# A fused encoder layer on one core: the order of the first transposes, of the first projection halves and of the parameter loads

## What is computed

```python
u = x @ w_in[l]                      # (1024 x 1024) @ (1024 x 7688)
ua, ub, uc, ug = _split(u, GROUP_COLS)
oa = _gdn_branch(ua, ...)            # gated delta rule, chunks of 64
ob, v_first = _rwkv7_branch(ub, ...) # RWKV-7 time mixing
oc = _swa_branch(uc, ...)            # sliding-window attention
merged = gates * (oa @ w_branch_a, ob @ w_branch_b, oc @ w_branch_c), summed
x = _layer_norm(ALPHA * x + merged @ w_out[l], ln1_w[l], ln1_b[l])
x = _layer_norm(ALPHA * x + (silu(x @ ffn_gate) * (x @ ffn_up)) @ ffn_down, ln2_w[l], ln2_b[l])
```

## Time and profile before

| | us |
|---|---|
| median of 3 runs | 2105.22 (2103.75 to 2105.71) |
| profiled execution, its time | 2102.6 |
| its span, first to last instruction | 2100.8 |
| TensorE busy | 1967.7 (94%) |
| VectorE busy | 1078.3 (51%) |
| ScalarE busy | 567.8 (27%) |
| GpSimd busy | 558.6 (27%) |
| mean granted TensorE clock | 0.974 of full speed |

### The profile page before, as it was taken

One profiled execution on the slowest core, in us unless ns is written; L12 is line 12 of the kernel. 1 busy time (PEld: TensorE's weight loads), 2 busy tenths in 40 slices (PEclk: granted clock), 3 DMA queues, 4 the chain that ended last, 5 costly groups with the idle time before them and its releaser, 6 DMA issues. The chain is left out here.

```text
span 2100.8 us, 29168 instructions
## 1 busy us (share of the span) xinstructions
PE 1967.7 (94%) x11664; PEld 1575.3 (75%) x11664; DVE 1078.3 (51%) x1354; ACT 567.8 (27%) x884; POOL 558.6 (27%) x353
## 2 busy tenths in 40 slices
PE   5998979999999999899888999999999999999994
PEld 4876758767788887777767777888888888888883
DVE  3665764468429900566657644724334243443437
ACT  2443332334421121333331121321121211212112
POOL 3111112121122322433314473422121221212113
PEclk9999989999999999899999999999999999999997
DMA  5243566135563393566464461211121211211002
GB/s 144 53 70 89 130 151 164 51 76 140 148 173 100 97 218 107 147 189 197 119 215 131 134 207 51 61 61 50 41 60 30 60 32 58 60 30 60 30 20 80
DMA packets 328054, 211.84 MB, mean 101 GB/s; under 512 B 154349, under 2 KB 298349, under 8 KB 325905
## 3 DMA queue, kind: packets, MB, share of 16 engines
q1 hardware_dynamic: 251760, 156.33, 27.3%
q10 hardware_dynamic: 75568, 54.04, 9.0%
q0 software_dynamic: 624, 0.05, 0.2%
HBM read 151.27 MB, written 59.06 MB: 100 GB/s over the span
## 5 line engine op out<-in xcount | busy, mean ns | idle before, releaser
L154 PE MATMUL bank<-xhi,w_hi 128*128 128x512 f32 x976 | 396.3, 406 | 2.9 <-DVE xlo L920 2.9
L155 PE MATMUL bank<-xlo,w_hi 128*128 128x512 f32 x976 | 387.6, 397 | 0.0
L156 PE MATMUL bank<-xhi,w_lo 128*128 128x512 f32 x976 | 387.0, 397 | 0.0
L432 POOL TENSOR_TENSOR w_lo<-w_raw,w_hi 128x1024 fp32r<-128x1024 f32 x61 | 163.3, 2678 | 640.5 <-ACT w_hi L783 640.5
L2212 DVE TENSOR_TENSOR bw_raw<-bw_raw,b_ps 128x512 f32<-128x512 f32 x42 | 28.9, 688 | 388.3 <-PE b_ps L156 380.0
L154 PEld LDWEIGHTS bank<-xhi,w_hi 128*128 128x128 f32 x976 | 184.9, 189 | 49.0 <-issue 3.5
L155 PEld LDWEIGHTS bank<-xlo,w_hi 128*128 128x128 f32 x976 | 185.0, 190 | 44.7 <-issue 2.4
L156 PEld LDWEIGHTS bank<-xhi,w_lo 128*128 128x128 f32 x976 | 184.6, 189 | 45.0
L2220 DVE TENSOR_TENSOR y<-y,f_ps 128x512 f32<-128x512 f32 x320 | 201.0, 681 | 0.7
L1755 POOL TENSOR_TENSOR bw_split<-ff_raw_down,ff_hi_down 128x1024 fp32r<-128x1024 f32 x22 | 53.4, 2426 | 527.3 <-ACT ff_hi_down L2013 527.3
L154 PE MATMUL f_ps<-ff_hi_down,ff_hhi 128*128 128x512 f32 x352 | 142.7, 405 | 3.6 <-DVE ff_hlo L2231 3.6
(11 more groups left out here) (324 smaller groups left out, 3462.6 us busy)
## 6 DMA issues: line engine op xcount, KB each, us to landing
w_raw<-in_w_in ACTq DMA_DIRECT2D x61, 512.0 KB, 4.2
op<-opnd SPq DMA_DIRECT2D x16, 1152.0 KB, 5.5
u<-work ACTq DMA_DIRECT2D x68, 256.0 KB, 4.1
b_gate<-u SPq DMA_DIRECT2D x24, 512.0 KB, 3.6
ff_raw_gate<-in_ffn_gate SPq DMA_DIRECT2D x22, 512.0 KB, 4.0
ff_raw_up<-in_ffn_up SPq DMA_DIRECT2D x22, 512.0 KB, 5.3
ff_raw_down<-in_ffn_down SPq DMA_DIRECT2D x22, 512.0 KB, 5.9
opnd<-work SPq DMA_DIRECT2D x20, 512.0 KB, 6.2
```

Source lines behind the costliest of these rows:

```text
L154: pe.matmul(out, w_hi, x_hi, start=first, stop=False)
L155: pe.matmul(out, w_hi, x_lo, start=False, stop=False)
L156: return pe.matmul(out, w_lo, x_hi, start=False, stop=last)
L432: pool.tensor_tensor(w_lo[b][:, :, :], w_raw[b][:, :, :], as_f32(w_hi[b][:, :, :]), ALU.subtract).then_inc(w_lo_done, 1)
```

## The change

On TensorE the first token half is transposed per token tile, each when it has landed, and only the last tile counts `turned`. `dense(0)` follows at once and waits for `xlo` block by block. The second half is transposed between `dense(0)` and `dense(1)`, in banks 3 to 7 only (`second_bank`), as banks 0 to 2 belong to the halves. On ScalarE `split(0)` moves ahead of all copies, and the second w tile's load behind `split(0)`. The 17 parameter loads move from GpSimd's queue to SP's, between x and the tables, and the tables get a semaphore of their own.

```diff
+        second_bank = lambda k: turn_bank[3 + k % 5]
...
-        rows_landed = sem("rows_landed")
+        rows_landed, tables_landed = sem("rows_landed"), sem("tables_landed")
...
         @block.gpsimd
         def _(pool):
-            nonlocal par_loads
-            par_loads = load_params(nc, pool, par, A, par_landed)
             for m in range(NT_IN):
...
-            pool.wait_ge(par_landed, par_loads)
             local.sweep(pool)
...
             for i in range(4, 8):
                 load_x(i)
-            sp.dma_start(tab.tile[:, P:], const_dram[:, P:N_TABLES]).then_inc(const_landed, 16)
+            par_loads = load_params(nc, sp, par, A, par_landed)
+            sp.dma_start(tab.tile[:, P:], const_dram[:, P:N_TABLES]).then_inc(tables_landed, 16)
             prep()
+            sp.wait_ge(par_landed, par_loads)
...
                 for k in range(KT):
+                    if q < 2:
+                        pe.wait_ge(x_lo_done, 8 * q + k + 1)
                     last = split_dot(pe, bank[to % 3][:, :], w_hi[b][:, k, :], w_lo[b][:, k, :],
...
             pe.wait_ge(const_landed, 16)
-            for n in range(16):
-                half, k = n // 8, n % 8
-                if k == 0:
+            for i in range(4):
+                pe.wait_ge(x_landed[i], 16)
+                for k in range(KT):
+                    last = pe.transpose(turn_bank[k][:, i * P:(i + 1) * P], work[:, i, k * P:(k + 1) * P], tab("ident"))
+                    if i == 3:
+                        last.then_inc(turned, 1)
+
+            def turn_second_half():
+                for i in range(4, 8):
+                    pe.wait_ge(x_landed[i], 16)
+                for k in range(KT):
+                    pe.wait_ge(x_lo_done, k + 4)
                     for i in range(4):
-                        pe.wait_ge(x_landed[4 * half + i], 16)
-                if n >= 8:
-                    pe.wait_ge(x_lo_done, n - 7)
-                for i in range(4):
-                    last = pe.transpose(turn_bank[n % 8][:, i * P:(i + 1) * P], work[:, 4 * half + i, k * P:(k + 1) * P], tab("ident"))
-                last.then_inc(turned, 1)
-            pe.wait_ge(x_lo_done, 16)
+                        last = pe.transpose(second_bank(k)[:, i * P:(i + 1) * P], work[:, 4 + i, k * P:(k + 1) * P], tab("ident"))
+                    last.then_inc(turned, 1)
...
                     dense(item)
+                    if item == 0:
+                        turn_second_half()
...
             load_w(0)
+            split(0)
             load_w(1)
             for n in range(16):
                 half, k = n // 8, n % 8
                 act.wait_ge(turned, n + 1)
-                act.activation(xhi[:, k, half * HALF:(half + 1) * HALF], turn_bank[n % 8], ACT.Copy).then_inc(x_hi_done, 1)
-                if n == 11:
-                    split(0)
+                act.activation(xhi[:, k, half * HALF:(half + 1) * HALF], second_bank(k) if half else turn_bank[k], ACT.Copy).then_inc(x_hi_done, 1)
             split(1)
...
-            dve.wait_ge(const_landed, 32)
+            dve.wait_ge(const_landed, 16)
+            dve.wait_ge(tables_landed, 16)
```

More of the change, by code:

```diff
@@ L571, in prep @@
                             sp.dma_start(out[:, :, which, 2 * r + pp, :], tile[64 * pp:64 * pp + 64, r, :, :]).then_inc(inv_stored, 16)
+            nonlocal par_loads
             load_x(0)
@@ L919, in _ @@
                 dve.wait_ge(x_hi_done, n + 1)
-                dve.tensor_tensor(xlo[:, k, cols_], turn_bank[n % 8], as_f32(xhi[:, k, cols_]), ALU.subtract).then_inc(x_lo_done, 1)
+                dve.tensor_tensor(xlo[:, k, cols_], second_bank(k) if half else turn_bank[k], as_f32(xhi[:, k, cols_]), ALU.subtract).then_inc(x_lo_done, 1)
             step(dve.memset(raws[:, :, 0:3], 0.0))
```

## The result

The changed kernel's median is 2083.56 us (2082.00 to 2084.76, four runs); the kernel before stood at 2104.49 beside it. The ratio is 0.9907 (95% interval 0.9895 to 0.9918): 0.93%, which is 19.6 us of 2104.49. (The two medians differ by 20.9 us, which the interval holds too.) The forecast was 2087.7 in a range from 2084 to 2097. The direction and the mechanism held and the gain was larger than forecast: the median of 2083.56 lies 0.4 us under the lower edge of the range, while the same ratio on the forecast's own base, 0.9907 x 2105.22 = 2085.6, lies inside it. The profiled execution's span went from 2100.8 to 2082.2.

The account below looks back on a forecast made before the run. TensorE, busy 94% of the span, was taken as the bound, its start waiting for x; q0 at 12.8 plus 5.6, 1.2 cold and 9.6 put q2 at 29.2 for 46.66, saving 17.5 us: 2087.7, range 2084 to 2097.

Parts of the forecast that it names:

- Arrival of x: Start of the kernel: with parameters behind x, tile 3 lands at 10.3 us and tile 7 at 16.7.
- own time only: Rival on x's landing: parameters cost x only their own 3.2 us; gain 13.1 us, 2092.1; chance 0.16.
- arrival unchanged: Rival on x's landing: x lands as before; gain 8.3 to 9.8 us, about 2096; chance 0.10.
- q0's start: First projection half on TensorE: starts at 12.8 us for 35.36, chosen between first x_lo (12.2) and w_lo (13.3).
- The term ahead of it: Transposes after x tile 3: ScalarE's first copy needs one transpose, not four; 0.5 us for 1.12.
- The clock: First projection half on TensorE: 1.2 us added for a part at 1.2 GHz, between nothing and 2.2.
- The second half's turn: Second token half's transposes, between the first two projection halves: q1 starts 4.0 us after q0 ends.
- The second w split: ScalarE and GpSimd ahead of q2: second w_lo is ready with 0.7 us to spare.
- Parameters late: Parameter loads on SP's queue behind x tile 7: landed at 28 us, ScalarE waits 2 us, no cost.
- a sign that it is wrong: Parameters on ScalarE: the forecast is wrong if ScalarE waits beyond 30 us for them.
- T + 9.7: ScalarE's next evacuation, by which it must be free of the parameter wait; T is q0's end, 19.6 us.
- 43: Rival on late parameters: landing between 43 and 53 us eats the gain to nothing; chance within 0.2%: 0.05.

Follow-up runs that it names:

- GpSimd experiment: Kernel before, with GpSimd waiting for all eight x tiles before it issues the parameter loads through its own queue; ratio 0.9999 (0.9989 to 1.0008).
- new order alone: Changed kernel with its parameter loads back on GpSimd's queue at the start; ratio to the kernel before 0.9949 (0.9935 to 0.9962), 10.7 us faster.
- tables experiment: Changed kernel with the tables ahead of the parameters on SP's queue; ratio to the kernel before 0.9908 (0.9893 to 0.9923).
- doubled loads: Changed kernel with every parameter load done twice on SP's queue; ratio to the kernel before 0.9982 (0.9973 to 0.9991), 3.8 us faster.
- first experiment: Kernel before with only the parameter loads moved to SP's queue behind x; ratio 0.9945 (0.9931 to 0.9958), 11.6 us faster.

## Why the prediction was right, point by point

- **Arrival of x.** 10.3 and 16.7 were forecast, 10.2 and 15.8 came. The reading of the earlier trace rows, that the parameters make x's rows dear, is shown by the GpSimd experiment, where they alone were moved in time. The "own time only" and "arrival unchanged" rivals fall with it. The traces have 72 engine-us per MB of x beside the loads on GpSimd's queue, and 40 to 41 with none beside it or with the same loads on ScalarE's, where about a ninth of them passed beside x. The Trainium skill ("DMA: Bandwidth & Descriptors", Issuing engines are not separate DMA queues) says that starting DMAs from several engines saves only the time to issue them. These traces don't agree: with the same loads started early, x tile 3 is there at 15.4 when they go through GpSimd's queue and at 10.44 when they go through ScalarE's.
- **q0's start.** 12.8 forecast, 12.84 measured, and that it is so close is luck. The 12.8 was chosen between a first x_lo at 12.2 and a w_lo at 13.3 at the latest. w_lo was there at 10.7 and didn't count; the first x_lo came at 12.7, 0.5 late, since TensorE was still transposing tile 2 at 1.2 GHz when tile 3 landed and turned to it at 10.95 only. The term ahead of it, 0.6 us for the order by token tile, was too small: undone, it costs 2.8 to 3.1. It left out that q0 itself stands behind the transposes on TensorE.
- **The clock.** This is the term of the sum that was mis-sized: 1.2 us were added for a cold part of q0 and there was none. The transposes' spacing fell from 0.21 to 0.11 us between 9.2 and 11.7, before any other matmul had run, so here they do raise the clock. The Trainium skill ("TensorE: Matmul & The Clock Gate", Part 4: PE-mode transpose) says that full clock doesn't engage for transposes. The trace contradicts it, and the trace decides. A cold q0 was no idle fear, though: with the new order alone, where x came more slowly, q0 did begin cold and took 7.3 us. The second half's turn took 3.6 us for 4.0. Against that q0 and q1 took 5.67 and 5.69 us for 5.6, 0.2 together, and q0 began 0.04 late. So 1.2 + 0.4 - 0.2 = 1.4 us, all by which the trace's 18.84 exceeds the 17.5.
- **The second w split.** Forecast 0.7 us ahead of q2; GpSimd finished at 26.6, 1.2 ahead of 27.82.
- **Parameters late.** 28 forecast, 32.8 measured. ScalarE waited 7.35 us where under 3 was forecast, and until past 30, which the prediction itself had named as a sign that it is wrong; on this step its mechanism was incomplete, and the time held because there was more room than it knew. The term took 0.75 us per 1,024 elements; from the end of x to the tail it was nearer 1, and the sinks' tail of 4 us and the held issue were not in it. The deadline was wrong too: it was set at T + 9.7 = 29.3, ScalarE's next evacuation, and the landing passed it by 3.5 us without any wait on TensorE. The first wait that counts is q4's on the third w_lo, 4.6 us behind the landing, so the deadline is 34.4 to 34.5 by the tables experiment, and the landing had 1.6 to 1.8 us left. From there on the gain shrinks, and not from 43. The point from which the kernel would turn slower than before (about 53) fits the doubled loads: 48.9 left 3.8 us of gain.
- **The rest of the difference.** The ratios give 19.6 and 20.0 us where the traces give 18.8 and 19.1. That is inside the intervals; whether something under a us more comes from elsewhere stays open. Two parts of the change, the first w split ahead of the copies and q0 between the two token halves, were never undone by themselves, so what each is worth isn't shown.

No version tried beats the changed kernel beyond what the runs can tell.

## What to carry to other kernels

When the first inputs of a kernel come late, look at what lies beside them on the DMA engines and who issued it, not at their bytes: 50 KB of single elements from GpSimd's queue cost x tile 3 some 5 us and tile 7 some 10 to 11 here. Then put the loads in the order in which they are wanted, and before adding to a queue find the first wait on what is moved back and its room; look at when a load of small rows lands beside one of large rows, as here its time changed from 6.5 us to 14.7 with the order of the issues. Where transposes feed matmuls, do them tile by tile as the tiles land; the matmuls stand behind them on the same engine.

## What was not expected of the hardware

- Loads of single elements issued by GpSimd nearly doubled the DMA time of rows of 4 KB from another queue (72 for 40 engine-us per MB). The same loads issued by ScalarE left them at 41, but only some 1,310 of 12,168 elements got through beside them. In the profiles the loads are 624 packets in GpSimd's queue before, and 12,416 more in SP's after (264,176 for 251,760).
- ScalarE's and SP's issue of a small load took up to 11.14 us when their queue held loads that drained slowly (8.59 in the changed kernel, 9.81 on ScalarE). An engine that has work of its own should not issue behind such loads.
- A w tile of 512 KB landed in 6.5 to 7.4 us in two profiles of the changed kernel and in 14.7 in one where a load of 64 KB had gone from SP's queue to ScalarE's, so that x beside it was issued 0.46 us earlier and the tile itself 0.45 later.
- After an idle stretch of 3.05 us TensorE's next matmuls began at full clock and lost it 1.3 us later (granted clock 0.50 from 25.3 to 27 in the first experiment); after 2.89 us in the kernel before they kept it.
